# Two buffers for the weight sums of the differential projection, another order of their transfers, and the first down product's low parts on GpSimd

## The reference, cut to what matters

```python
for l in range(DEPTH):                                  # DEPTH = 2
    h = rms_norm(x, norm_g[l]) * (1.0 + scale) + shift
    gq, gk, gv, glr, gz, dq, dk, dv, dz = split_columns(h @ w_in[l])
    ...
    o_diff = diff_branch(dq, dk, dv, dz, ...)           # 4 heads, q and k normed, softmax, gated by silu(dz)
    x = x + gate * (concat(o_gla, o_diff) @ w_out[l])
...
u = causal_dwconv(h @ ffn_w_up, ffn_conv_w) + ffn_conv_b
gate, up = split(u, 2)
x = x + rms_norm_2((silu(gate) * up) @ ffn_w_down, norm_ffn_post)
```

## Time and profile before

| | before |
| --- | --- |
| median of 3 runs | 2386.41 us (2385.91 to 2389.37) |
| the profiled execution: time, span | 2387.8 us, 2386.1 us |
| PE busy (L856, L1693, L4304, L4369 and others) | 2297.6 us, 96% of the span |
| DVE, ACT, POOL busy | 1424.2, 1101.5, 642.5 us |
| DMA, share of 16 engines over the span | 27.5% (queue q1), 226.72 MB moved in all |
| mean granted clock of TensorE | 0.987 of full |

### The profile page before, as it was taken

The page is one execution under the profiler, slowest core; times in us unless marked ns, Lnnn a source line. Parts: engine busy times, 40 slices in busy tenths (PEclk is TensorE's granted clock), DMA queues, the critical chain, the costliest instruction groups (busy, mean ns, idle before and its releaser), DMA issues. The chain is left out here.

```text
span 2386.1 us, 33486 instructions
## 1 busy us (share of the span) xinstructions
PE 2297.6 (96%) x12692; PEld 1872.3 (78%) x12692; DVE 1424.2 (60%) x1934; ACT 1101.5 (46%) x2350; POOL 642.5 (27%) x448
## 2 busy tenths in 40 slices
PE   7999997999999999989999999999999999999998
PEld 4887776778887777777888887677878888887887
DVE  5955433885553532586553166562487788786757
ACT  4444314674544432476442545553653333334653
POOL 2200011133310012033232112111214444545752
PEclk9999998999999999999999999999999999999999
DMA  7432241104212233002211100003222332326864
GB/s 255 150 122 75 86 180 36 37 1 146 84 44 74 69 124 141 18 19 86 100 62 47 58 1 5 14 19 115 89 75 82 117 115 93 106 88 233 280 194 159
DMA packets 160772, 226.72 MB, mean 95 GB/s; under 512 B 10684, under 2 KB 104291, under 8 KB 159077
## 3 DMA queue, kind: packets, MB, share of 16 engines
q1 hardware_dynamic: 159573, 224.58, 27.5%
q10 hardware_dynamic: 1040, 0.00, 0.0%
HBM read 176.05 MB, written 48.50 MB: 94 GB/s over the span
## 5 line engine op out<-in xcount | busy, mean ns | idle before, releaser
L856 PE MATMUL ps<-w_hi,hT_hi 128*128 128x512 f32 (+1 forms) x384 | 144.0, 375 | 9.3 <-POOL w_lo L787 7.2
L787 POOL TENSOR_TENSOR w_lo<-difp_raw,w_hi 128x2048 fp32r<-128x2048 f32 x8 | 36.6, 4572 | 429.7 <-ACT w_hi L756 429.7
L4247 POOL TENSOR_TENSOR w_lo<-ffn_sums,w_hi 128x512 fp32r<-128x512 f32 x76 | 96.8, 1296 | 183.7 <-DVE hT_raw L4639 116.4
L856 PE MATMUL ps<-w_hi,hT_lo 128*128 128x512 f32 (+1 forms) x384 | 143.7, 374 | 0.0
L856 PE MATMUL ps<-w_lo,hT_hi 128*128 128x512 f32 (+1 forms) x384 | 143.7, 374 | 0.0
L856 PE MATMUL ps<-hT_hi,w_hi 128*128 128x512 f32 x360 | 140.5, 390 | 0.0
L856 PE MATMUL ps<-hT_lo,w_hi 128*128 128x512 f32 x360 | 140.0, 389 | 0.0
L856 PE MATMUL ps<-hT_hi,w_lo 128*128 128x512 f32 x328 | 127.7, 389 | 0.0
L4304 PE MATMUL ps<-ffn_t_hi,w_hi 128*128 128x512 f32 x304 | 118.4, 389 | 0.9 <-DVE ffn_u L4626 0.9
L4304 PE MATMUL ps<-ffn_t_hi,w_lo 128*128 128x512 f32 x304 | 118.3, 389 | 0.0
L4304 PE MATMUL ps<-ffn_t_lo,w_hi 128*128 128x512 f32 x304 | 118.3, 389 | 0.0
(11 more groups left out here) (624 smaller groups left out, 6613.9 us busy)
## 6 DMA issues: line engine op xcount, KB each, us to landing
ffn_raw<-in_ffn_w_up SPq DMA_DIRECT2D x40, 512.0 KB, 4.6
mix_gla<-in_w_ada SPq DMA_DIRECT2D x32, 512.0 KB, 3.5
xres<-big SPq DMA_DIRECT2D x24, 512.0 KB, 2.6
parts<-in_ffn_w_down SPq DMA_DIRECT2D x22, 512.0 KB, 4.7
wsum<-parts SPq DMA_DIRECT2D x11, 1024.0 KB, 3.8
ffn_sums<-hsum SPq DMA_DIRECT2D x44, 256.0 KB, 4.5
ffn_raw<-wsum SPq DMA_DIRECT2D x44, 256.0 KB, 5.0
glap_raw<-in_w_in SPq DMA_DIRECT2D x10, 1024.0 KB, 5.2
```

What stands on the lines that cost most here:

```text
L787: pool.tensor_tensor(m.w_lo[:, b, 0:w], raw[:, 0:w], m.w_hi[:, b, 0:w].bitcast(F32), ALU.subtract).then_inc(s_lo, 1)
L856: mm = nc.tensor.matmul(out, l, r, start=(job.part != 1 and c == 0 and k == 0), stop=(job.evac and c == job.chunks - 1 and k == len(pairs) ...
L4247: pool.tensor_tensor(lo, op.source(n), hi.bitcast(F32), ALU.subtract).then_inc(s_lo, 1)
```

## The change

In the differential projection `parts` becomes two buffers, each with its own load and store semaphore. `move` is split into `load(n)` and `store(n)`, and SP runs a fixed list: behind tile 1 load 0, load 1, store 0, load 2, store 1, load 3; behind tile 2 store 2, load 4, store 3, load 5; behind tile 3 store 4, store 5 and a wait for all stores; nothing behind tile 4. The buffers' memory is given back before `keys_and_norm`.

In the feed-forward part POOLED goes from 6 to NK = 11: POOL makes the right low parts of steps 6 to 10 too, and DVE begins at 11. SP issues the loads of steps 11 to 15 ahead of the last two stores; the load of `w_post` and two row loads behind it move by one or two steps. In the first Winograd round `feature_sums(0)` and `feature(2)` go behind the adds that signal `s_e` and `s_c22`, and POOL waits for `feature_sums(0)` before the low part of product 1 of round 1.

```diff
     def enter(self, nc, ctx, m):
-        self.buf = ctx.enter_context(m.tensor("parts", [P, 4, 512], F32))
+        self.bufs = [ctx.enter_context(m.tensor(f"parts{b}_", [P, 4, 512], F32)) for b in range(2)]
...
+    def load(self, sp, n):
+        if n >= 2:
+            sp.wait_ge(self.s_store[n % 2], 16 * (n // 2))
+        for i in range(2):
+            c = self.ks[n] + FFN // P // 2 * i
+            sp.dma_start(self.bufs[n % 2][:, 2 * i:2 * i + 2, :],
+                         self.w_down[P * c:P * c + P, :].rearrange("p (h n) -> p h n", h=2)).then_inc(self.s_load[n % 2], 16)
+    def store(self, sp, n):
         k = self.ks[n]
...
         sp.wait_ge(self.s_sum, 4 * (n + 1))
         sp.dma_start(self.wsum[P * k:P * k + P, :].rearrange("p (s n) -> p s n", n=512),
-                     self.buf[:, :, :]).then_inc(self.s_store, 16)
-        if n == len(self.ks) - 1:
-            sp.wait_ge(self.s_store, 16 * (n + 1))
+                     self.bufs[n % 2][:, :, :]).then_inc(self.s_store[n % 2], 16)
+    def move(self, sp, t):
+        for verb, n in ((), ("l0", "l1", "s0", "l2", "s1", "l3"), ("s2", "l4", "s3", "l5"), ("s4", "s5"), ())[t]:
+            if int(n) < len(self.ks):
+                (self.load if verb == "l" else self.store)(sp, int(n))
+        if t == 3:
+            for b in range(2):
+                sp.wait_ge(self.s_store[b], 16 * len(range(b, len(self.ks), 2)))
...
     def sp_job(sp, q, t):
-        for n in range(2 * t - 2, 2 * t):
-            if 0 <= n < len(parts.ks):
-                parts.move(sp, n)
+        parts.move(sp, t)
...
-    STAGED, POOLED, RING, AHEAD, LAST = 5, 6, 16, 12, 6
+    STAGED, POOLED, RING, AHEAD, LAST = 5, NK, 16, 12, 6
...
-            for n in range(4, NK):
+            for n in range(4, NK + 5):
                 load_left(n)
                 load_right(n)
             store(NF - 1)
             store_feature_sums(NK - 1)
-            for n in range(NK, NDOWN):
+            for n in range(NK + 5, NDOWN):
...
+                if s == 1 and k == 1:
+                    pool.wait_ge(s_fsum, 4)
...
-                if s == 0:
-                    feature_sums(0)
-                feature(j - 1)
+                if s:
+                    feature(j - 1)
                 if s + 1 < NWINO:
                     weight_sums(s + 1)
                 dve.wait_ge(s_prod, NPROD * s + 4)
                 add(u_half(1, 1), u_half(1, 0), s, 1, s_e)
                 dve.wait_ge(s_e, s + 1)
                 add(u_half(1, 1), u_half(1, 1), s, 2, s_c22)
+                if s == 0:
+                    feature_sums(0)
+                    feature(j - 1)
```

More of the change, by code:

```diff
@@ L1550, in enter @@
     def enter(self, nc, ctx, m):
-        self.buf = ctx.enter_context(m.tensor("parts", [P, 4, 512], F32))
-        self.s_load, self.s_sum, self.s_store = semaphores(nc, ctx, m, "parts", "load sum store")
-    def move(self, sp, n):
-        k = self.ks[n]
[L1557 to L1562, removed]
+        self.bufs = [ctx.enter_context(m.tensor(f"parts{b}_", [P, 4, 512], F32)) for b in range(2)]
+        self.s_sum, *self.s_load = semaphores(nc, ctx, m, "parts", "sum load0 load1")
+        self.s_store = semaphores(nc, ctx, m, "parts", "store0 store1")
+    def load(self, sp, n):
[6 more added lines that the diff above has]
+    def store(self, sp, n):
+        k = self.ks[n]
         sp.wait_ge(self.s_sum, 4 * (n + 1))
         sp.dma_start(self.wsum[P * k:P * k + P, :].rearrange("p (s n) -> p s n", n=512),
-                     self.buf[:, :, :]).then_inc(self.s_store, 16)
-        if n == len(self.ks) - 1:
-            sp.wait_ge(self.s_store, 16 * (n + 1))
+                     self.bufs[n % 2][:, :, :]).then_inc(self.s_store[n % 2], 16)
[6 more added lines that the diff above has]
+                sp.wait_ge(self.s_store[b], 16 * len(range(b, len(self.ks), 2)))
     def sums(self, dve, n):
-        b11, b12, b21, b22 = (self.buf[:, i, :] for i in range(4))
-        dve.wait_ge(self.s_load, 32 * (n + 1))
+        b11, b12, b21, b22 = (self.bufs[n % 2][:, i, :] for i in range(4))
+        dve.wait_ge(self.s_load[n % 2], 32 * (n // 2 + 1))
         dve.tensor_tensor(b11, b12, b11, ALU.subtract).then_inc(self.s_sum, 1)
@@ L1590, in groups, with tail @@
         return ap.rearrange("p (g d) -> p g d", d=DIFF_DH)
+    summing = ExitStack()
+    def tail(ctx, block, q):
+        summing.close()
+        keys_and_norm(nc, ctx, block, m, q, jobs[-1], qk, ssq, base, start)
     def setup(ctx, q):
         q.sq = ctx.enter_context(m.tensor("difp_sq", [P, 2, DIFF_W], F32))
-        parts.enter(nc, ctx, m)
+        parts.enter(nc, summing, m)
     def sp_job(sp, q, t):
-        for n in range(2 * t - 2, 2 * t):
-            if 0 <= n < len(parts.ks):
-                parts.move(sp, n)
+        parts.move(sp, t)
     def dve_before(dve, q):
@@ L1629, in stage_diff_project @@
                   lambda job: "AV" if job.tag == "q" else "A", extra="sq sum moved", setup=setup, ready=1, base=base,
-                  act_before=act_after_first, sp_job=sp_job, dve_before=dve_before, block=block,
-                  tail=lambda ctx, block, q: keys_and_norm(nc, ctx, block, m, q, jobs[-1], qk, ssq, base, start))
+                  act_before=act_after_first, sp_job=sp_job, dve_before=dve_before, block=block, tail=tail)
 def keys_and_norm(nc, ctx, block, m, q, job, qk, ssq, base, start):
@@ L4217, in _ @@
             store_feature_sums(NK - 1)
-            for n in range(NK, NDOWN):
+            for n in range(NK + 5, NDOWN):
                 load_left(n)
                 load_right(n)
-                if n == NK + 3:
+                if n == NK + 5:
                     sp.dma_start(sg[:, :], w_post).then_inc(s_w, 16)
-                if n in (NK + 5, NK + 7):
-                    load_row((n - NK - 5) // 2)
+                if n in (NK + 6, NK + 7):
+                    load_row(n - NK - 6)
                 if n == NK + 9:
```

## The result

The changed kernel takes **2356.86 us** (median of four runs, 2353.90 to 2359.27), the kernel before on the same chip 2387.89 us (four runs, 2385.91 to 2389.86). The ratio is 0.9869, with a 95% interval of 0.9852 to 0.9887. The forecast was 2357.5 us. The two medians lie 31.0 us apart, where 28.9 had been forecast: the kernel before ran 1.5 us above the median that the forecast started from. The profiled execution took 2359.27 us, its span 2357.5, where 2358.9 and 2357.2 had been forecast. Two executions further down (one of ten of the new feed-forward part alone, 3797 us, and one of sixteen of the kernel before beside it, 4065 us) had a mean granted clock of 0.56 and 0.73 and are left out of every comparison.

A forecast was written before the change was run, and what follows sets the result against it. PE, busy 96% of the span, bounds the kernel, so only its waits can gain: projection 24.9, Winograd round 1.1, seam 2.9, together 28.9 us off 2386.4, giving 2357.5 us; range 2354.5 to 2365.5 (forecast's own 2355 to 2360).

The forecast's parts named there:

- Layer 0: Differential projection, layer 0: job 0 to the keys' second tile falls from 120.27 to 102.0 us, gain 18.27 us.
- signs of being wrong: Stop before job 2, clock under 0.9 between the jobs, or new PE waits on DMA in the down product.
- the issue of tile 2: SP's list in the projection: tile 2 goes out at 292.7 to 295.9, ready 13.7 us later, against a need of 312.7.
- rival (a): Projection: tile 2 comes late behind store 1 or load 3 and PE stops, 2361 to 2373 us; chance 0.13.
- Layer 1: Differential projection, layer 1: its stop of 3.96 us, costing 6.65 with the clock, goes; gain 6.65 us.
- rival (e): Projection: SP's waits merely move the lateness to tile 4, only the feed-forward part gains 4 us, 2382; chance 0.04.
- (d): Projection: overlapping loads and stores take whole extra serial rounds, kernel slower, two rounds give 2405 us; chance 0.03.
- The Winograd round: First Winograd round: moving DVE's sums removes PE's 0.85 us stop, gain 1.1 us; POOL's new wait costed at nothing.
- The seam: Down product: POOL's added low parts remove the stop before step 6, gain 2.9 us (bounds 0.9 and 3.2).
- the 0.3 of loss: Down product: expected cost at step 11, right part 11 alternating with POOL on DVE, ready about level with the need.
- rival (b): Down product: step 11 waits 2.3 us or more on DVE, clock falls, 2360 to 2363 us; chance 0.10.
- The page's rule: Last convolution: DVE freed after one POOL operation, gain 3.2 in place of 2.9, total 2357.2 us; chance 0.04.

## Why the prediction was right, and where its steps were off

**The sum is closer than its terms.** The span fell by 28.6 us against 28.9. Layer 0 gave 1.6 less than forecast and the Winograd rounds 0.5 less, and the 1.6 of the untouched stretch, which is chance, made up for most of it. Without that luck the gain is 27.0 us, still inside the range. Two of the prediction's own signs of being wrong did appear, both small: a stop before job 2 (0.58 us) and a clock under 0.9 between the jobs (0.57 over 4 us).

**Layer 0: the mechanism held, 1.6 us too much.** The stops of 3.26 and 8.05 went and only the 1.84 and its neighbour stayed, as layer 1 had shown. The forecast was 102.0 us from job 0 to the keys' second tile; 103.54 was measured. The mis-sized term is the issue of tile 2: I put it at 292.7 to 295.9, bounding store 1 at 7.0 us by a tile that had a store ahead of it. A store with a load ahead of it took 9.4 us here (7.7 to 8.8 in other places), so tile 2 went out at 298.90. Its 13.7 us from issue to use grew too, to 14.6. That is rival (a), in its mildest form: 0.9 us in layer 0 with the spacing (88.01 to the first matmul of k0, against 87.14 in layer 1), nothing in layer 1, where store 1 took 7.8. The other 0.7 is the clock: I had counted no fall behind the 1.9, by layer 1, and in layer 0 it fell. The kernel run again took 103.60 with 1.7 us lost on tile 2 and no fall, and 103.60 - 1.7 is 101.9, the forecast: so the sum of the rest was right. I had named the late tile 2, and priced it at 5 us over my later bound; store 1 was 2.4 over the bound, which the slack took almost whole.

**Layer 1: right.** 6.72 against 6.65, 101.93 us against 102.0. The step that a stop of 3.96 costs 6.65 with the clock is confirmed by its removal, for this pair of executions: with the old projection profiled once more (the feed-forward part alone) the stop was 4.12, the clock 0.72 over 6 us in place of 0.60, and the layer took 107.90 us, so the stop cost 6.0. Tile 3 went out 19.8 us behind tile 2 in layer 0, forecast 14 to 22; at 318.68 it was 0.7 behind my latest bound and 2.1 ahead of the need.

**The order is what gains: right.** The old order on two buffers gave back 16 us and rival (e) with it; (d), slower, needed whole serial rounds more, while overlap cost a store only 4 to 6 us (7.7 to 9.9 in place of the 3.8 of the earlier trace rows). The second buffer alone gave some 6.5.

**The Winograd round: 0.6 in place of 1.1, and the mis-sized term is the wait that I had cost at nothing.** The stop of 0.85 went, but POOL's row, held back by the wait, then met DVE's taps, two of which took 1.30 and 2.20 instead of 0.75 and 1.28, and a stop of 0.3 us stands at 1807.23. The timelines of DVE and of PE in the kernel after:

```profile
1801.50 1.30 DVE L4604 TENSOR_SCALAR ffn_sg<-ffn_u,fcols 128x1024 f32<-128x1024 f32 x1
1802.84 2.20 DVE L4606 SCALAR_TENSOR_TENSOR ffn_sg<-ffn_u,fcols,ffn_sg 128x1024 f32<-128x1024 f32 x1
```

```profile
1807.23 0.50 PE L4320 MATMUL ps<-ffn_t_hi,w_hi 128*128 128x512 f32 x1 [0.29 <-DVE ffn_u L4642]
```

The wait itself pays: without it 4.0 us are lost. I had looked only at who waits behind it, not at what POOL's row would meet on DVE with it or without it.

**The seam: 3.2 in place of 2.9.** The hold came as predicted, 14.27 us against 14.3, and moved `feature` by what POOL's row grew. Right part 11 took 1.78 us, the alternation I had chosen as the nearer row; it started at 2168.88 and ended at 2170.66, and the need was 2141.9 + 11 x 2.72 = 2171.8, so PE wasn't stopped and the 0.3 of loss was not there. What the prediction named but didn't price is what this rests on: step 11 can afford the hold only since its operands are loaded ahead of the stores. With the loads late the hold costs 5.4 us in an execution that has it. That is the outcome of rival (b) by another path, since PE then waits for POOL and not for DVE. Nor did it price the clock behind the stop of 2.96: where the old seam was profiled again it fell, and the down product took 213.9 us, so the seam is worth 3.2 to 4.7.

**The page's rule** (the Trainium skill, SBUF — State Buffer, "Who interferes with whom": of a GpSimd and a VectorE operation on the shared ports the second is blocked until the first finishes) gave 2357.2 us, which the time can't tell from 2357.5. The rows can: the operation stood through eleven operations of POOL in the kernel after, not through one, and it stood through the whole row in ten of the twelve profiles in which no wait kept POOL away (8.0 us with the old feed-forward part, 14.2 to 14.8 with the new one). The rule describes the other two, 1.77 and 1.78 us: the rest of one operation of POOL, 1.2 us, and then some 0.6 of its own. With POOL's wait in place it took 1.79 and 1.80, in both profiles.

**What stays open.** Why the operation stands in most executions and slips through in others, of one and the same kernel too (1.77 and 14.23, on different chips, but each chip showed both behaviours). The distance from the start of POOL's operation to its own doesn't tell them apart: 0.07 and 0.05 us where it slipped, 0.05 to 0.09 where it stood. Nor is it known why `tensor_tensor` takes turns with POOL in the feature sums but not here; the size (128x1024 against 128x512) wasn't tried. And the moved sums of the first Winograd round weren't priced apart from POOL's wait: without it the new place lost 4.0 us, and the old place with it wasn't run.

## What to carry to other kernels

Where loads and stores share a queue with work that is due, write down which entry each entry truly waits for: a load that waits for a buffer holds everything issued behind it, so put what is due ahead of it, and judge a second buffer by the order that it allows too: here the buffer alone gave some 6.5 us, the order 16.9. When an operation is moved to another engine, look at what its row will meet on the engine that works beside it, not only at who waits for it: here one such meeting cost 14 us of DVE and none of PE, because the operands had been loaded early, and a wait that seemed idle was worth 4 us. Before a gain of one or two microseconds is believed, look at how much the same stretch differs between executions of unchanged code: here up to 3.9 us.

## What the runs showed of the hardware

- One DVE operation of 0.75 us stood for 14.23 to 14.27 us while POOL ran operation behind operation, and ended 0.54 to 0.56 behind the last (made a `tensor_tensor`: 14.79, and 1.09 behind); in between POOL kept its 1.25 us a piece. Other DVE operations took turns with POOL at 1.67 to 1.78 us each. With a wait of 0.63 us on POOL it was done in 1.79 and 1.80.
- A store of 1 MB took 3.8 to 4.2 us alone in the queue, 7.7 to 9.4 with 1 MB of load issued just ahead of it.
- Behind one and the same stop of 1.84 us the granted clock over the next 4 us was 1.00 in 13 of 18 cases (both layers of the nine profiled executions that have it behind the new order), and 0.57 to 0.69 in the other five, of one and the same kernel too. The fall cost 0.6 to 1.0 us in four of them and 2.8 in the fifth.
